# Who carries the sixteen blocks of a turned gated product in a two-layer transformer kernel: GpSimd's transfers alone, or GpSimd and ScalarE

## What is computed

```python
def _swiglu(x, w_gate, w_up, w_down):
    return (jax.nn.silu(x @ w_gate) * (x @ w_up)) @ w_down
...
x = x + 0.5 * _swiglu(_rmsnorm(x, ffn1_norm[l]), ffn1_w_gate[l], ffn1_w_up[l], ffn1_w_down[l])
...
x = x + (g[:, :, 0] * y_a + g[:, :, 1] * y_b + g[:, :, 2] * y_c) @ w_out[l]
x = x + 0.5 * _swiglu(_rmsnorm(x, ffn2_norm[l]), ffn2_w_gate[l], ffn2_w_up[l], ffn2_w_down[l])
```

## Time and profile before

| what | us |
|---|---|
| median of three launches (lowest to highest) | 1137.66 (1136.94 to 1138.67) |
| the profiled execution, its own time | 1136.88 |
| its span, first to last instruction | 1135.1 |
| TensorE busy | 1127.0 |
| VectorE busy | 913.8 |
| ScalarE busy | 692.1 |
| GpSimd busy | 350.6 |

### The profile page before, as it was taken

One profiled execution on the slowest core, in us unless ns is written; L12 is line 12 of the kernel. 1 busy time (PEld: TensorE's weight loads), 2 busy tenths in 40 slices (PEclk: granted clock), 3 DMA queues, 4 the chain that ended last, 5 costly groups with the idle time before them and its releaser, 6 DMA issues.

```text
span 1135.1 us, 15393 instructions
## 1 busy us (share of the span) xinstructions
PE 1127.0 (99%) x5425; PEld 923.1 (81%) x5425; DVE 913.8 (80%) x1230; ACT 692.1 (61%) x961; POOL 350.6 (31%) x669
## 2 busy tenths in 40 slices
PE   9999999999999999999999999999999999999997
PEld 7888888888777888888888888888877788888886
DVE  6997876878977698888589888577898696987884
ACT  6766655457764477566467657554677635665653
POOL 3526251062000054333435252602410000634432
PEclk9999999999999999999999999999999999999999
DMA  9998784795325877967797967757943349779681
GB/s 325 302 342 267 215 264 144 233 272 185 132 75 186 289 235 208 359 182 242 247 308 218 342 204 226 235 175 214 279 156 110 140 127 330 233 243 340 168 277 54
DMA packets 165788, 257.77 MB, mean 227 GB/s; under 512 B 18528, under 2 KB 95184, under 8 KB 164688
## 3 DMA queue, kind: packets, MB, share of 16 engines
q1 hardware_dynamic: 144928, 234.81, 62.4%
q0 software_dynamic: 20096, 21.27, 8.7%
q10 hardware_dynamic: 688, 0.71, 0.2%
HBM read 234.45 MB, written 1.05 MB: 207 GB/s over the span
## 4 chain that ended last, share of the span: by engine, by line
PE 97%; ACT 1%; DMA 1%; DVE 0%; issue 0%; POOLq 0%; POOL 0%; SPq 0%; DVEq 0%; ACTq 0%
PE ps L1760 25%; PE ps L1761 25%; PE ps L1762 25%; PE ps L1892 4%; PE ps L1893 4%; PE ps L1894 4%; PE ps L2006 2%; PE ps L2062 2%; PE ps L2034 2%; PE ps L1810 2%; PE ps L1779 1%; DMA raw<-in_w_in_dram 1%; ACT whi L1443 1%; PE ps L1977 0%; PE ps L2185 0%
## 5 line engine op out<-in xcount | busy, mean ns | idle before, releaser
L678 DVE TENSOR_TENSOR wlo<-raw,whi 128x2048 fp32r<-128x2048 f32 (+1 forms) x187 | 417.4, 2237 | 116.0 <-ACT whi L1443 71.0
L1443 ACT ACTIVATE whi<-raw 128x2048 fp32r<-128x2048 f32 (+1 forms) x187 | 350.5, 1878 | 156.7 <-PE ps L1762 99.3
L1760 PE MATMUL ps<-whi,ht_hi 128*128 128x512 f32 (+1 forms) x936 | 366.0, 391 | 0.5 <-DVE wlo L678 0.4
L1762 PE MATMUL ps<-whi,ht_lo 128*128 128x512 f32 (+1 forms) x936 | 361.2, 386 | 0.0
L1761 PE MATMUL ps<-wlo,ht_hi 128*128 128x512 f32 (+1 forms) x936 | 360.8, 385 | 0.0
L571 POOL DMA_DIRECT2D act_blocks<-act_blocks x288 | 141.8, 501 | 232.1 <-DVE act_blocks L746 230.2
L1760 PEld LDWEIGHTS ps<-whi,ht_hi 128*128 128x128 f32 x936 | 175.9, 188 | 36.5 <-issue 2.5
L1762 PEld LDWEIGHTS ps<-whi,ht_lo 128*128 128x128 f32 x936 | 175.8, 188 | 36.1
L1761 PEld LDWEIGHTS ps<-wlo,ht_hi 128*128 128x128 f32 x936 | 176.0, 188 | 33.4
L571 POOL DMA_DIRECT2D gated_all<-gated_all x240 | 117.8, 501 | 81.2 <-DVE gated_all L746 78.6
L1405 POOL TENSOR_SCALAR gates<-gates 128x512 f32<-128x512 f32 x24 | 21.9, 930 | 174.6 <-ACT gates L1611 174.6
(11 more groups left out here) (224 smaller groups left out, 1656.0 us busy)
## 6 DMA issues: line engine op xcount, KB each, us to landing
raw<-in_ffn_w_down_dram SPq DMA_DIRECT2D x88, 512.0 KB, 5.4
raw<-in_w_in_dram SPq DMA_DIRECT2D x88, 512.0 KB, 4.6
raw<-in_ffn_w_gate_dram SPq DMA_DIRECT2D x85, 512.0 KB, 4.7
raw<-in_ffn_w_up_dram SPq DMA_DIRECT2D x69, 512.0 KB, 5.8
T_raw<-in_ffn_w_up_dram SPq DMA_DIRECT2D x32, 512.0 KB, 6.8
T_raw<-in_ffn_w_gate_dram SPq DMA_DIRECT2D x32, 512.0 KB, 9.1
T_raw<-T_raw POOLq DMA_DIRECT2D x8, 1024.0 KB, 9.0
raw<-in_w_out_dram SPq DMA_DIRECT2D x16, 512.0 KB, 4.5
```

The costliest lines, as they stand in the source:

```text
L678: nc.vector.tensor_tensor(wlo[:, n, 0:w], raw[:, n, 0:w], whi[:, n, 0:w].bitcast(F32), ALU.subtract).then_inc(lo_done, 1)
L1443: nc.scalar.activation(whi[:, n, 0:w], raw[:, n, 0:w], ACT.Copy).then_inc(hi_done, 1)
L1760: nc.tensor.matmul(o, xh, wh, start=start, stop=False)
L1762: return nc.tensor.matmul(o, xl, wh, start=False, stop=stop)
```

## The change

`CROSSING` now begins with the four blocks (a, a), so that GpSimd issues sixteen transfers per step and the four that stay in their quarter come first. `landed` counts them through `carried`, so `act_round` waits for sixteen. ScalarE's `pass_on` does nothing below `LATE`, and the wait on `act_kept_early` is gone. `products` on VectorE gets a wait for the transposes issued before it: they read `act`, which it overwrites; that order came before by way of ScalarE's copies.

```diff
             else:
-                eng.wait_ge(act_kept_early, (r * LATE + i + 1) * 4)
+                pass
...
-        CROSSING = [(a, q) for a in range(4) for q in range(4) if a != q]
+        CROSSING = [(a, a) for a in range(4)] + [(a, q) for a in range(4) for q in range(4) if a != q]
...
+            turns_issued = [0]
+
             def products(l, f, i):
 
                 r = l * 2 + f
+                if turns_issued[0]:
+                    dve.wait_ge(act_turned, turns_issued[0])
...
                 ins.then_inc(act_turned, 1)
+                turns_issued[0] += 1
...
             def pass_on(l, f, i):
 
-                if i < LATE:
-                    keep_act(l, f, i)
-                else:
+                if i >= LATE:
                     cross_act(eng, l, f, i, BY_ACT, act_crossed)
```

## The result

The changed kernel takes 1155.25 us (median of five launches, 1154.49 to 1155.73), the kernel before in the same comparison 1137.40 (1136.71 to 1138.67). The ratio is 1.0156, with a 95% interval of 1.0144 to 1.0168: 17.9 us slower, where 11.9 were predicted. It is inside the range, 0.25 us from its upper end. The profiled span is 1153.4 us, 18.3 over the one before.

A forecast was written before the change was run, and what follows sets the result against it. TensorE, busy 99% of the span, was taken as the bound, so only new TensorE waits cost time: 3 x 3.65 + 0.9 = 11.9 us on 1137.66 gives 1149.5 us, range 1143.0 to 1155.5.

The forecast's parts named there:

- D: Delay of the last landing of step 10, at each feed forward's end: 4.0 us taken at three, 1.96 at the last.
- the price D - 0.35: How late TensorE ends at each of the first three feed forwards' ends: 3.65 us each.
- the last end's 0.9: Cost in the last feed forward, where no slab is loaded: 1.96 - 1.09 = 0.9 us.
- Nothing for ScalarE, nothing for steps 0 to 9: Some 57 us of removed ScalarE copies worth nothing in the chain; later transfers in steps before 10 hidden, 0 taken.
- 6% of more DMA: Added blocks, 4 x 16 KB beside each 1 MB slab; up to 0.5 us in the first feed forward, 0 taken.
- The wait on VectorE in `products`: Added wait for the transposes of the step before, done by then: 0 taken, at most under 1 us a step.
- By that the last block lands at 173.35 + 5.1: First feed forward's end, step 10: last block lands 5.1 us after the loads' issue, at 178.45, giving D = 3.7.
- The loads move too: Step 9's last block lands 0.6 us later, so loads go at 173.95, last block lands at 179.05: D = 4.3.
- the upper bound of 5.8: Upper end of D at step 10, from 5.5 us issue to landing, halfway between the median and the longest.
- Rival 3: TensorE's clock falls in the new waits of about 3 us, 6 us more in three places: 1155.7 us; chance 0.08.
- Rival 1: Step 10's landing is undisturbed because slab loads go earlier: D = 1.96, 5.7 us slower, 1143.4 us; chance 0.23.
- Rival 2: Not slower: GpSimd issues the four blocks at almost no cost, 1137.7 us; chance 0.07 together with a fourth rival.

The follow-up runs named there:

- kernel 1: Changed kernel with ScalarE's copies back in step 10 only, GpSimd carrying all sixteen blocks in steps 0 to 9: 1137.86 us, ratio 1.0002.
- kernel 2: Changed kernel with ScalarE's copies back in steps 0 to 9, GpSimd carrying all sixteen blocks in step 10 only: 1152.09 us, ratio 1.0127.
- kernel 6: kernel 1 with ScalarE's copies also in steps 0 to 3 of the first feed forward: 1138.02 us, ratio 1.0004.
- kernel 9: Changed kernel with unread matmuls in TensorE's wait before down 10: twelve at the first and third end, twenty at the second: 1153.45 us, ratio 1.0143.
- kernel 3: Changed kernel with the slab loads beside step 10's last blocks held until its `act_rest`, in the first three ends: 1144.64 us, ratio 1.0063.
- kernel 8: Changed kernel with two of the four slab loads at the second end going out one step later: 1153.20 us, ratio 1.0140.
- kernel 5: Changed kernel with the order turned round, the twelve blocks that change quarter first, the four that stay last: 1154.54 us, ratio 1.0147.
- kernel 4: Changed kernel with twelve unread matmuls in TensorE's wait before down 10 in the first three feed forwards: 1153.14 us, ratio 1.0136.

## Why the prediction was right, and where its sizes were off

**Right:** direction, place and mechanism. The bound, the four waits before down 10, the issue of 0.49 us each, 1.96 at the last end (D 1.96), and the price D - 0.35 of the first three ends all stand. Of the 11.9 us, the last end's 0.9 measured 1.15 and the third end's 3.65 measured 3.7, the latter with some luck (below).

**Nothing for ScalarE, nothing for steps 0 to 9:** right within what can be measured as long as step 10 is left alone (kernel 1); together with step 10's blocks they bear on when the loads go out (kernel 2). ScalarE lost 51 us, where the prediction had some 57. Its 6% of more DMA is misread: a step has three slabs of 1 MB, beside which 64 KB are 2%. It was only the start that had a term of up to 0.5 us beside the 0 taken. The profile shows 0.9, kernel 6 is no faster than kernel 1, and this stays open. The wait on VectorE in `products` shows nowhere in the waits of TensorE.

**Off, D.** The step that failed is "By that the last block lands at 173.35 + 5.1": the nearest row was a first block 2 us behind the loads of a burst, and I carried its 5.1 us over to the last of several. Measured, it lands 5.95 to 6.1 us after the loads' issue with two of them and 7.5 us with four, and D was 4.35, 5.81 and 4.09 against the 4.0 taken. A second step failed the other way, "The loads move too": it took the median 3.7 us for the landing of step 9's last block, which took 2.8, and had the loads go out 0.6 us later. Counted from GpSimd's first transfer of step 10 they went out 0.3 to 0.5 us earlier (5.27 us at the first end against 173.35 - 167.72 = 5.63 before). At ends 1 and 3 the two errors nearly cancel, so that D came within 0.35 us of 4.0 there is in part luck. Most of the error is the second end, where the prediction let one pattern stand for three. SyncE's queue of the kernel before, of which the prediction used the first end alone, has two loads more at the second:

```profile
558.24 0.37 SPq L2208 DMA_DIRECT2D raw<-in_ffn_w_gate_dram  x1
558.65 0.51 SPq L2208 DMA_DIRECT2D raw<-in_ffn_w_up_dram  x1
559.20 1.02 SPq L2254 DMA_DIRECT2D T_raw<-in_ffn_w_up_dram  x2
```

That the upper bound of 5.8 is the value measured where four loads stand is chance: it was made from the spread of all landings, not from four loads. Against the profiled execution the sum lacks 18.3 - 11.9 = 6.4 us: 2.3 are D (0.35 + 1.81 + 0.09), 3.0 the clock, 0.9 the start, 0.3 the last end (with rounding).

**Off, the clock.** Rival 3 was given 0.08 and came true on top of the forecast in two of three ends. It was priced at 6 us with half of 18 matmuls in each of three places; in the changed kernel 20 slow matmuls in two places cost some 3.0 us. Its total, 1155.7, is close to the 1155.25 measured by chance: of its 6 us over the forecast 3.0 were the clock, and the rest were D, the start and the last end. A cost of that kind is no rival to a wait but its companion: where the forecast itself makes waits of 3 us, a chance of the clock falling belongs into the forecast's own sum. The Trainium skill (TensorE: Matmul & The Clock Gate, Part 1) has the clock drop to half when TensorE idles, and the traces agree: 1.00 to 0.50 behind waits, and 1.00 kept in kernel 9 where these are filled.

**The rivals.** Rival 1's number, 1143.4, is what kernel 3 gives (1144.6), but not for its reason: with early loads, in kernel 2, the blocks still take 3.3 us. Only held loads make it true. Rival 2 is refuted: the added transfers cost GpSimd 501 ns each like the others, and kernel 3, in which little but the issue is left, is 7.0 us slower than before. The Trainium skill (DMA: Bandwidth & Descriptors, section Anatomy of one DMA — SWDGE path) says that many descriptors can be emitted before the extra cost shows. What was added here are whole transfers, of 16 KB in 32 rows, and four of them cost 1.96 us of issue, so the prediction's reading of that rule, D near 0, does not hold; no run varies the descriptors within a transfer.

## What to carry to other kernels

A transfer that is last in a queue and waited for is priced by what else is in flight when it goes out, so list the loads beside each repeat of the place, not beside the first. If a helper engine's queue is on the path, more items in it cost their full issue time, even when another engine is freed by it: the same four blocks on a second queue cost nothing here. And a new TensorE wait of 2 to 5 us can cost 1 to 2 us more than its length, in some ends and not in others.

## What was not expected of the hardware

- **The length of a wait does not say whether the clock falls.** It stayed after 2.7 us (changed kernel, end 3) and after 3.3 (kernel 8, end 2), and fell after 2.2 (kernel 2, end 1), 2.7 and 2.8 (kernel 8, ends 1 and 3), 2.8 (kernel 5, end 3), 3.0 and 4.4 (changed kernel) and even after 1.9 behind 2.8 us of unread matmuls (kernel 4, end 2). One and the same kernel does not repeat itself either: the mean clock of kernel 2's launches goes from 0.994 to 0.998, with 2.5 us between their times. What decides was not settled; no run here varied it by itself.
- **It also falls for different lengths:** 5 to 8 matmuls or 12 to 13, about 1 or about 2 us, with nothing between in these ten falls.
- **The loads' effect lasts:** a block of 16 KB issued 3.2 us after the first of two loads (1 MB in all) still lands twice as late as one with nothing beside it (3.3 against 1.6 us).
